# Sample attention of a hybrid encoder step: another order of score and value products

## The reference

```
A: z = q.k / 8;  a = exp(log_sigmoid(z) + suffix sum of log_sigmoid(-z))    stick-breaking
B: p = softmax(q.k / 8 + g_key - g_query)                                   forgetting
C: p = softmax(q.k / 8 over the top-k keys that an indexer selects)         sparse
y = sum over branches of sigmoid(gate_n) * (o_n @ w_branch_n);  out = y @ w_out
```

## Time and profile before

| | us |
|---|---|
| median of three runs | 2450.82 |
| span of the profiled execution | 2448.7 |
| TensorE busy | 2368.4 |
| VectorE busy | 1230.5 |
| ScalarE busy | 564.4 |
| sample attention, layer 0 | 139.40 |
| sample attention, layer 1, stretch read | 138.00 |

### The profile page before, as it was taken

How to read it: one execution, slowest core, us unless ns; L and a number is a source line. 1 busy time by engine, 2 the same in 40 slices (tenths; PEclk the granted TensorE clock), 3 DMA queues, 4 the chain that set the end, 5 groups by cost and what they waited for, 6 DMA issues and landing times.

```text
span 2448.7 us, 41369 instructions
## 1 busy us (share of the span) xinstructions
PE 2368.4 (97%) x17088; PEld 2041.6 (83%) x17088; DVE 1230.5 (50%) x2612; ACT 564.4 (23%) x1308; POOL 154.0 (6%) x292
## 2 busy tenths in 40 slices
PE   7999999999998999999999999999999989999998
PEld 6999996875665589999999999878756655999998
DVE  3656522634665426565265662335165844366742
ACT  3000022114554222001130000311235431410011
POOL 0000000000037100000000000000000560000000
PEclk9999999999999999999999999999999999999999
DMA  8454343862389442542335533357435893323232
GB/s 321 136 186 153 98 150 111 260 214 85 117 272 319 136 164 101 186 148 95 129 114 187 182 117 119 135 159 267 151 102 173 284 291 120 111 80 128 95 117 74
DMA packets 299916, 390.85 MB, mean 160 GB/s; under 512 B 33773, under 2 KB 245609, under 8 KB 299730
## 3 DMA queue, kind: packets, MB, share of 16 engines
q1 hardware_dynamic: 275746, 333.91, 40.8%
q0 software_dynamic: 16896, 45.43, 5.7%
q10 hardware_dynamic: 7088, 8.87, 1.0%
HBM read 378.54 MB, written 9.62 MB: 159 GB/s over the span
## 4 chain that ended last, share of the span: by engine, by line
PE 85%; DMA 4%; DVE 3%; ACT 2%; SPq 2%; POOL 1%; issue 1%; ACTq 0%; DVEq 0%; POOLq 0%
PE PS L677 29%; PE PS L775 12%; PE PS L982 6%; PE PS L1219 4%; PE PS L930 4%; PE PS L876 3%; PE PS L647 2%; PE PS L823 2%; PE PS L831 2%; PE PS L952 2%; PE PS L716 2%; PE PS L1241 2%; DMA BIG<-w_ada 2%; PE PS L1233 2%; PE PS L1129 2%; PE PS L1104 1%
## 5 line engine op out<-in xcount | busy, mean ns | idle before, releaser
L677 PE MATMUL PS<-OT,RING 128*128 128x192 f32 x1280 | 234.2, 326 | 0.0
L677 PE MATMUL PS<-H,RING 128*128 128x192 f32 x1280 | 223.4, 328 | 0.0
L677 PE MATMUL PS<-OT,QR 128*128 128x192 f32 x1280 | 221.1, 326 | 0.0
L677 PEld LDWEIGHTS PS<-OT,RING 128*128 128x128 f32 x1280 | 212.4, 190 | 0.0
L677 PEld LDWEIGHTS PS<-H,RING 128*128 128x128 f32 x1280 | 208.4, 190 | 4.4 <-issue 4.1
L677 PEld LDWEIGHTS PS<-OT,QR 128*128 128x128 f32 x1280 | 210.2, 190 | 0.0
L1347 ACT ACTIVATE QR<-QR 128x384 f32<-128x384 f32 x80 | 41.8, 523 | 530.9 <-DVE QR L1916 530.9
L982 PE MATMUL PS<-H,RING 128*128 128x384 f32 x480 | 160.9, 490 | 0.0
L982 PEld LDWEIGHTS PS<-H,RING 128*128 128x128 f32 x480 | 89.1, 190 | 61.5 <-issue 4.7
L1694 POOL DMA_DIRECT2D QR<-cache_sb_v x16 | 12.9, 804 | 1728.2 <-DVE QR L2249 1652.3
L677 PE MATMUL PS<-H,QR 128*128 128x192 f32 x640 | 117.1, 326 | 0.0
(11 more groups left out here) (305 smaller groups left out, 4164.9 us busy)
## 6 DMA issues: line engine op xcount, KB each, us to landing
RING<-ffn_w_in SPq DMA_DIRECT2D x80, 1024.0 KB, 7.3
RING<-w_in SPq DMA_DIRECT2D x64, 768.0 KB, 6.2
QR<-w_ada SPq DMA_DIRECT2D x34, 1024.0 KB, 10.0
BIG<-w_ada SPq DMA_DIRECT2D x34, 1024.0 KB, 10.2
RING<-ffn_w_out SPq DMA_DIRECT2D x32, 768.0 KB, 4.6
RING<-ffn_w_out SPq DMA_DIRECT2D x32, 640.0 KB, 5.4
QR<-cache_sb_v POOLq DMA_DIRECT2D x16, 768.0 KB, 6.2
QKT<-cache_sb_k SPq DMA_DIRECT2D x16, 768.0 KB, 6.4
```

Of the source, the lines that this page charges most:

```text
L677: mm = pe.matmul(PS[:, bank, GROUP[g]], a[:, k, :], x[:, k, :], start=(k == 0), stop=(k == 3))
```

## The change

- Value products move from unit s-1 at the end of step s to unit s-2 directly behind the scores of unit s; output moves from unit s-2 to s-3. There are two more steps at the end instead of a written-out tail. The masked rows (OU) get a second buffer, the softmax statistics four columns instead of two.
- TensorE turns the fourth key group first and the three others behind it, both after the probabilities; the fourth goes into bank 3 in all units. A key buffer is released only by the second of the two (turn_three).
- A gate piece is 8 steps of the contraction over 192 tokens instead of 4 steps over 384. It stands last in the step, in bank 3, and waits for ScalarE's copy of the fourth group; ScalarE copies each half.
- The new keys' probabilities go to bank 4, beside the scores, and wait until VectorE has read the scores of unit s (sz_taken). Scores wait until the new probabilities of unit s-2 have been copied (sn_copied).
- In the six stick-breaking units ScalarE copies the turned probabilities (PROBS_ACT).
- VectorE takes the maximum right behind the bias, then copies the output, masks the value rows, and copies probabilities. The selection's rounds are spread anew: none in step 3, three in steps 7 and 9, one in step 8.

```diff
-ROUND_S = {0: 1, 1: 2, 2: 2, 3: 1, 4: 2, 5: 2, 6: 1, 7: 2, 8: 2, 9: 2}
+ROUND_S = {0: 1, 1: 2, 2: 2, 4: 2, 5: 2, 6: 1, 7: 3, 8: 1, 9: 3}
...
+GATE_HALVES = len(GATE_UNIT) // 2
...
+def last_part(s):
+    before = [u for u in GATE_UNIT if u < s]
+    return GATE_UNIT[max(before)] if before else None
...
-        OU = NORM[:, (PC + 1) * P:(PC + 2) * P]
+        OU = [NORM[:, (PC + 1) * P:(PC + 2) * P], AR[:, :]]
...
-                        u, i = last_unit(n - KBUF)
-                        sp.wait_ge(kt_ready, 2 * (l * NSTEP + u) + 1 + i // 3)
+                        u, _ = last_unit(n - KBUF)
+                        sp.wait_ge(kt_ready, 2 * (l * NSTEP + u) + 2)
...
+                def part_copied(s):
+                    if last_part(s):
+                        n, half = last_part(s)
+                        if half:
+                            pe.wait_ge(gate_taken, l * 24 + n + 1)
+                        else:
+                            pe.wait_ge(half_taken, l * GATE_HALVES + n - GATE_FIRST_UNIT)
+                def turn_fourth(s):
+                    pe.wait_ge(kt_free, 3 * (l * NSTEP + s) + 1)
+                    part_copied(s - 2)
+                    turn_group(s, 3, 3).then_inc(kt_ready, 1)
...
+                def gate_part(s):
+                    n, half = GATE_UNIT[s]
+                    r = R_GATE + n // 3 - 1
+                    if half == 0 and n % 3 == 0:
+                        full(l, r)
+                    part_copied(s)
+                    if s + 2 < NSTEP:
+                        pe.wait_ge(kt_free, 3 * (l * NSTEP + s + 2) + 2)
+                    w = ring(l, r, KD, MIX)
+                    for k in range(KD):
+                        mm = pe.matmul(PS[:, 3, 0:HALF], w[:, k, (n % 3) * P:(n % 3 + 1) * P], H[:, k, GROUP[half]],
+                                       start=(k == 0), stop=(k == KD - 1))
+                    mm.then_inc(gate_ready if half else half_ready, 1)
+                def scores(s):
+                    pe.wait_ge(kt_free, 3 * (l * NSTEP + s) + 4)
+                    if l or s:
+                        pe.wait_ge(sz_taken, l * NSTEP + s)
                     if s >= 2:
-                        pe.wait_ge(kt_free, 3 * (l * NSTEP + s) + 2)
-                    turn_group(s, 3, 3 if s < 2 else 0).then_inc(kt_ready, 1)
-                def gate_half(n, half):
-                    r = R_GATE + n // 3 - 1
-                    if half == 0:
-                        if n % 3 == 0:
-                            full(l, r)
-                        pe.wait_ge(gate_taken, l * 24 + n)
-                    w = ring(l, r, KD, MIX)
-                    for k in range(4 * half, 4 * half + 4):
-                        mm = pe.matmul(PS[:, 3, 0:T], w[:, k, (n % 3) * P:(n % 3 + 1) * P], H[:, k, :],
-                                       start=(k == 0), stop=(k == KD - 1))
-                    if half:
-                        mm.then_inc(gate_ready, 1)
+                        pe.wait_ge(sn_copied, l * NSTEP + s - 1)
+                    for half in range(2):
+                        for i, (n, a) in enumerate(unit_groups(s)):
+                            mm = pe.matmul(PS[32 * i:32 * i + 32, 4 + half, 0:264], QBLK[:, n // NB, a, n % NB, :],
+                                           KT[s % 2][:, i, half * 264:(half + 1) * 264], start=True, stop=True)
+                    mm.then_inc(ss_ready, 1)
...
+                def values(s):
+                    for n in sorted({n for n, _ in unit_groups(s)}):
+                        pe.wait_ge(v_full[n % VBUF], l * (NCACHE // VBUF * 32) + 32 * (n // VBUF + 1))
+                    pe.wait_ge(ou_ready, l * NSTEP + s + 1)
+                    if l or s:
+                        pe.wait_ge(o_free, l * NSTEP + s)
+                    pe.wait_ge(st_copied, l * NSTEP + s + 1)
+                    pe.wait_ge(sn_copied, l * NSTEP + s + 1)
+                    for c in range(PC + 1):
+                        k = P if c < PC else NT
+                        for i, (n, a) in enumerate(unit_groups(s)):
+                            v = VC[n % VBUF][:, c, a * P:(a + 1) * P] if c < PC else VN[n % VBUF][0:NT, a * P:(a + 1) * P]
+                            mm = pe.matmul(PS[32 * i:32 * i + 32, 7, 0:P], PTS[0:k, c, i * 32:(i + 1) * 32], v,
+                                           start=(c == 0), stop=(c == PC))
+                    mm.then_inc(pv_ready, 1)
...
                 def output(s):
                     pe.wait_ge(ou_ready, l * NSTEP + s + 2)
                     settle(pe)
-                    pe.matmul(PS[:, 7, P:P + UNIT * NT], OU, OWN_ROW, start=True, stop=True).then_inc(o_ready, 1)
+                    pe.matmul(PS[:, 7, P:P + UNIT * NT], OU[s % 2], OWN_ROW, start=True, stop=True).then_inc(o_ready, 1)
...
                 def turn_new_probs(s):
-                    pe.wait_ge(o_free, l * NSTEP + s + 1)
-                    pe.transpose(PS[0:NT, 7, 2 * P:3 * P], ES[s % 2][:, PAST:KEYS], IDENT[:, :]).then_inc(st_ready, 1)
...
+                    if s + 1 < NSTEP:
+                        pe.wait_ge(sz_taken, l * NSTEP + s + 2)
+                    pe.transpose(PS[0:NT, 4, 3 * P:4 * P], ES[s % 2][:, PAST:KEYS], IDENT[:, :]).then_inc(st_ready, 1)
                 def step(s):
-                    pe.wait_ge(kt_free, 3 * (l * NSTEP + s) + 4)
-                    pe.wait_ge(zs_ready, l * NSTEP + s + 2)
...
+                    if s < NSTEP:
+                        scores(s)
+                    if 2 <= s:
+                        values(s - 2)
+                    if s >= 3:
+                        output(s - 3)
+                    if 1 <= s <= NSTEP:
                         turn_probs(s - 1)
-                    if s + 2 < NSTEP:
-                        turn_three(s + 2)
-                    if s >= 1:
                         turn_new_probs(s - 1)
-                    if s in GATE_UNIT:
-                        gate_half(*GATE_UNIT[s])
-                    if s >= 1:
-                        values(s - 1)
                     if s + 2 < NSTEP:
                         turn_fourth(s + 2)
+                        turn_three(s + 2)
+                    if s in GATE_UNIT:
+                        gate_part(s)
...
                 def turned_three(s):
                     g = s % NU * UNIT
-                    act.wait_ge(kt_ready, 2 * (l * NSTEP + s) + 1)
+                    act.wait_ge(kt_ready, 2 * (l * NSTEP + s) + 2)
                     A(KT[s % 2][:, 0:3, 0:PAST], PS[:, 0:3, :], ACT.Copy).then_inc(kt_free, 1)
                     A(KT[s % 2][:, :, PAST:KEYS], KNT[s // NU][:, g:g + UNIT, :], ACT.Copy).then_inc(kt_free, 1)
...
+                def take_part(s):
+                    n, half = GATE_UNIT[s]
+                    if half:
+                        act.wait_ge(gate_ready, l * 24 + n + 1)
+                    else:
+                        act.wait_ge(half_ready, l * GATE_HALVES + n - GATE_FIRST_UNIT)
+                    A(G[:, n, GROUP[half]], PS[:, 3, 0:HALF], ACT.Copy).then_inc(gate_taken if half else half_taken, 1)
                 def step(s):
                     e = ES[s % 2]
-                    p = s % 2
-                    begin()
-                    if s + 1 < NSTEP:
-                        turned_fourth(s + 1)
-                    if s >= NU and s + 2 < NSTEP:
+                    p = s % 4
+                    if s < NSTEP:
+                        begin()
+                        act.wait_ge(zs_ready, l * NSTEP + s + 3)
+                        if s < NU:
+                            link(A(LS, ZS, ACT.Sigmoid, scale=-1.0))
+                            A(e, ZS, ACT.Sigmoid).then_inc(es_ready, 1)
+                        else:
+                            A(e, ZS, ACT.Exp, bias=ST[:, p:p + 1], accum_out=ST[:, 8 + p:9 + p]).then_inc(es_ready, 1)
+                    if PROBS_ACT and 1 <= s <= NU:
+                        act.wait_ge(st_ready, 2 * (l * NSTEP + s - 1) + 1)
+                        if s >= 2:
+                            act.wait_ge(pv_ready, l * NSTEP + s + 1)
+                        A(PTS[:, 0:PC, :], PS[:, 6, :].rearrange("p (c q) -> p c q", q=P), ACT.Copy).then_inc(st_copied, 1)
+                    if s + 2 < NSTEP:
+                        turned_fourth(s + 2)
                         turned_three(s + 2)
-                    act.wait_ge(zs_ready, l * NSTEP + s + 3)
-                    if s < NU:
-                        link(A(LS, ZS, ACT.Sigmoid, scale=-1.0))
-                        A(e, ZS, ACT.Sigmoid).then_inc(es_ready, 1)
-                    else:
-                        A(e, ZS, ACT.Exp, bias=ST[:, p:p + 1], accum_out=ST[:, 8 + p:9 + p]).then_inc(es_ready, 1)
-                    if s < NU and s + 2 < NSTEP:
-                        turned_three(s + 2)
-                    if s in GATE_UNIT and GATE_UNIT[s][1]:
-                        take_gate(GATE_UNIT[s][0], 3)
+                    if s in GATE_UNIT:
+                        take_part(s)
...
                 def turned_probs(s):
```

(45 more changed lines are left out.)

69 lines of the change are left out of this document (16 added, 53 removed).

## The result

The changed kernel takes 2474.3 us (median of 4 runs, 2467.8 to 2477.63) against 2450.07 us (4 runs) of the kernel before beside it: ratio 1.009, 95% interval [1.0078, 1.0101]. It is slower by 24 us, outside the range that I gave; the slow rival had named the mechanism, and even its 2462 us was too low.

A forecast was written before the change was run, and what follows sets the result against it. TensorE was taken to bound the sample attention, with DMA close behind. Gains of 36.0 us against costs of 34.5 us gave net -1.5 us, 2449.3 us beside the median of 2450.8; range 2435 to 2461.

The forecast's parts named there:

- slow rival: TensorE before the fourth group of units 3, 6, 9, 12, 15: key waits replace removed ones; +11.5 us, 2462 us; chance 0.19.
- Order waits: TensorE's waits in values, output and new-probability transpose, 24.0 us in both layers, mostly go: 17.7 us gained.
- the mask's 4.8: Part of the new-probability transpose's wait put to the late mask: 4.8 us, taken out and priced anew among the costs.
- Width changes: TensorE's switches between narrow and full-width products fall from four to two a step: 9.6 us gained, bounds 0 and 13.4.
- Gate pieces: On TensorE, 16 instructions over 192 tokens replace 8 over 384 per piece: 0 us, bounds -0.04 and +0.3 us a piece.
- Key buffers: TensorE waits for key loads released late and needed one step later, the decisive term: 22 us lost, range 7 to 36.
- five units: Units 3, 6, 9, 12, 15, whose fourth group starts a new cache: 18.1 us of waits, landings taken a microsecond shorter.
- caches 15 and 23: Key loads needed earlier in their units as well: 0 to 8 us more waiting, taken as 4 us.
- Clock: TensorE at half clock behind long waits: two stretches instead of one, +2.9 us, range -2.9 to +8.7 (four).
- Mask: Sparse branch's mask arrives late for the bias addition, met in the new-probability transpose: 4 us lost, range 0 to 6.4.
- small waits: Gate piece waits for ScalarE's fourth-group copy, scores of steps 13 and 17 for the new-probability copy: 5.6 us, range 3 to 8.
- "faster" rival: Key loads that matter land in 5 us, mask wait 2 us, no late pair: net -13.4 us, 2437.4 us; chance 0.34.

The follow-up runs named there:

- e1: Changed kernel, but the fourth key group of units 0, 3, 6, 9, 12, 15 is turned from the cache before (wrong keys): 2451.36 us, ratio 1.000.
- e8: Changed kernel, but each of the three key groups signals by itself, so some buffers are released earlier: 2464.05 us, ratio 1.0049.
- e4: Kernel before, with one edit: a key buffer is released only by the second turn of its unit: 2479.54 us, ratio 1.0116.
- e3: Changed kernel with the fourth key group last again, behind the gate piece, and the release of the kernel before: 2445.4 us, ratio 0.9979.
- e7: e1 with value products moved behind the transposes of the probabilities, apart from the scores: 2501.68 us, ratio 1.0194.
- e2: Changed kernel with 18 filler instructions ahead of the fourth key group of units 6, 9, 12, 15, results unchanged: 2465.68 us, ratio 1.0059.
- e9: e3 with each unit's bias brought by one broadcast load (one or two for the mask) instead of eight: 2454.59 us, ratio 1.0012.

## Why the prediction was wrong

The steps in its order; "measured" is the profiled execution.

1. **Order waits, 17.7 us gained plus the mask's 4.8 taken out: right.** Of 24.0 us, 1.9 us stay in output, 0.93 per layer (I said 0.8). Gain 22.1 us, against my 22.5.
2. **Width changes, 9.6 us gained: some 7.6.** Scores and values take 2.25 us together after, 2.40 before (1.03 + 1.37), which is 0.15 x 32 = 4.8 us. The whole stages show more: TensorE's busy time grew by 127.28 - 123.61 + 128.66 - 124.19 = 8.1 us, though half clock alone added 18.8 - 3.1 = 15.7. The rest of the work therefore got 7.6 us shorter. Part of it is the fourth key group, which no longer stands alone between values and scores (before, 4 products took 0.58 us; at 752.43 the 16 take 1.84 us start to start, 0.46 for four). The Trainium skill (TensorEngine Tiling (Array Packing), Key Properties) says that a mode change drains the engine. The gain of 7.6 us over 32 steps, 0.24 us each, is smaller than the loader's 0.42 us gap; the price of a drain by itself was not isolated.
3. **Gate pieces, 0: about right.** 16 products take 2.70 us start to start at full clock (746.65 to 749.35 above) against 2.67, under 1 us in all.
4. **Key buffers, 22 us: the step that failed, with 5.** The five units were right, and so were the distances but for unit 3 (6.2 us instead of 4.5). The size was not. My 22 us were 18.1 us for the five units and 4 us for caches 15 and 23. Those two show no wait, and the five show 35.7 us, twice the 18.1. I had made each landing a microsecond shorter, "since a waiting TensorE also starts fewer transfers". They were about a microsecond longer (8.0 us in the mean of the eight loads of units 6, 9, 12 and 15, 6.7 before). With the landings as they stood in the rows, the sum of the five would have been 28.1 us, nearer. e1 takes the early need away, and with it 23 us of the loss; e8 gives 11 us less waiting for 0.9 to 1.6 us more distance at each place. Why the landings grew is open: e4 has the same pairs of loads, and its first loads landed in 5.8 us.
5. **Clock, +2.9 us: a second failure of size.** I allowed two half-clock stretches, four at most; there are eight, one per unit of 6, 9, 12, 15 and layer. The eight groups of 16 transposes take 3.41 to 3.65 us, 28.8 together, instead of 8 x 1.91, which makes 13.5 us; scores or gate pieces behind some of them make the rest, 18.8 us in all, 15.7 more than the single stretch before. Having worked out waits of 2 to 4 us at five places a layer, I should have charged half clock at each of them: in the trace of before the 2.9 us wait had it and the 2.5 us wait had not. The Trainium skill (TensorE: Matmul & The Clock Gate, "HAM oscillation") says that repeated idle gaps between bursts keep sending the clock down; eight of eight waits of 2.8 us and more agree here, and one of 3.03 us in e8 does not. The rule was in my text, but not in my sum.
6. **Mask, 4 us, and small waits, 5.6 us: right in size.** 2.2 us at the new-probability transpose, 3.4 + 2.7 = 6.1 us at scores and gate pieces. But in e1 and e3 the mask and bias wait is 12 to 14 us as soon as the key waits go, twice my upper bound of 6.4, which was for the mask alone. My "faster" rival, with 2 us for it, would have met it too.

The sum with what was measured: 22.1 (order waits with the mask's part) + 7.6 (shorter work) + 3.9 (old key waits) = 33.6 us gained, 35.7 + 2.2 + 6.1 + 15.7 = 59.7 us lost, net +26.1 us. The span says +25.5. The 7.6 is what remains of the busy time, so the closing sum shows that waits, clock and work are all counted, not what made the work shorter.

Steps 4 and 5 feed on each other: a long wait costs its length and about 2 us more of slow work. That made the outcome lopsided, which my chances (0.23 for slower) did not say. So the miss is not luck: both sizes erred to the same side, and 17.6 us at the five units and 12.8 us of clock are more than the 27 us of span between forecast and result.

Not tried: the early turn of the fourth group without the rest of the change, a change of width priced by itself, ScalarE's copies alone, and fewer bytes on the queues.

## What to carry to other kernels

When steps are put close together, work out for every buffer the time from its release to its next need, and set it against the landing times seen under that very load, not against shorter ones; a release signal that comes with a later group takes its delay off that time, and if it frees two buffers at once, the second load lands later too (e4). Add the half-clock work behind a long TensorE wait to its length: here 33.3 us of waits at eight places cost 18.8 us more. And a wait that is removed may only have covered the next one: here 12 to 14 us of bias waits came up once the key waits were gone.

## What the runs showed of the hardware

- Half clock doesn't follow from the length of one wait alone: eight of eight waits of 2.83 to 5.75 us had it after the change, but in e8 a wait of 3.03 us was followed by 16 transposes in 1.94 us, and in e7, with a wait of 1.5 us in nearly every step, one of them was followed by 16 in 3.42 us and the one before it by 16 in 1.97 us.
- Extra work in place of waiting made the kernel faster (e2: 24 us of products whose result is not used, 8.6 us saved).
- Of two 768 KB loads issued 0.5 us apart, the second landed late: 12.7 us in the mean of eight in e4, against 9.1 where the two went out 2.6 to 7.3 us apart; the first landed in 5.8 us.
- One broadcast load of 264 KB landed in 9.2 us and eight of 33 KB took 10.0 us from the first issue to the last landing (medians), but with the one load the key loads of the forgetting and the sparse branch landed 1.2 and 1.8 us later (e9 against e3).
